# The first 16 tiles of the conditioning product: the conditions stationary in four column groups, the weights moving

## The chip, the cores and the metric

The kernel runs on one core of a Trainium2 chip. The metric is the device time of one execution in microseconds (us), the median of three runs. The core's engines are TensorE (PE; PEld is its weight load), VectorE (DVE), ScalarE (ACT), GpSimd (POOL) and SyncE (SP), which here issues most of the loads from HBM.

## What is computed

One inference step of a two-layer decoder trunk, for a prompt of 256 tokens and 8 samples of one token each (264 columns in all). Cut to the part in question:

```python
for l in range(DEPTH):                                   # DEPTH = 2
    mod = jax.nn.silu(c) @ W['w_mod'][l] + W['b_mod'][l] # c: (1 or 8, 1024), w_mod[l]: (1024, 6144)
    sh1, sc1, g1, sh2, sc2, g2 = split(mod, 6)
    h = rmsnorm(x, W['mix_pre_g'][l]) * (1 + sc1) + sh1
    z, xbc, dt_raw, u, v, ga, gb = split_cols(h @ W['w_in'][l], IN_SIZES)
    ...                                                  # SSD branch, gated MLP branch, merge
    x = x + g1 * rmsnorm(merged @ W['w_o'][l], W['mix_post_g'][l])
    h = rmsnorm(x, W['ffn_pre_g'][l]) * (1 + sc2) + sh2
    ...                                                  # dense (l = 0) or top-2-of-8 channel mixer (l = 1)
```

Everything is float32. The first 16 tiles of 128 columns of `w_mod[0]` give `sh1` and `sc1` of layer 0, and without them the first `h` can't be formed.

## The kernel before, in words

Activations lie with the features on the 128 partitions (8 tiles of 128 features, 264 columns). The large products split every weight chunk of 1024 by 256 into a high part (ScalarE, `split_hi`) and a low part (VectorE, `split_lo`), and TensorE multiplies the parts with those of the activations in `pe_phase` (lines 367, 368, 374). Each engine has its own program; semaphores tie them together, and each engine works through its program in the order in which it is written. There is no planner: the order is written out by hand.

The front of the kernel is what stands before the first of these products.

- SyncE loads the 9 conditions into `ctok`, then 8 pieces of `w_mod[0]`, each 1024 rows by 256 columns (1 MB, runs of 1 KB), into buffers that are free at that time (`START`: `zs`, `ub`, `vb`, `sga`, `sgb`, `hf` and two of the `raw` ring). After them on the same queue come the first two chunks of `w_in`; the third waits until VectorE has made the low part of chunk 0.
- ScalarE's queue loads x as rows of tokens; GpSimd's queue loads the parameter rows, the convolution state and small tables.
- TensorE turns the conditions (line 733), and ScalarE copies them to `cT` (line 1227). Then comes a loop over the 8 pieces. For each piece, `unit` (line 771) computes two tiles: for each of 8 row blocks the 128 by 128 block of `w_mod` is stationary and the ten condition columns, repeated up to 12 times, move. Between the pieces stand the transposes of x, of the parameters and of the states (`turn`, lines 748 to 760) and, after the seventh piece, the sum of squares for the first norm (`norm(1)`, line 716). All of that is one sequence on TensorE.
- VectorE copies each turned tile from PSUM (line 1577). When x is complete, ScalarE squares it; after the sum comes the root (ScalarE, line 1211), the reciprocal (VectorE, line 1515) and the scaling of x (line 1581).
- VectorE then takes the 16 tiles' sums from PSUM (`take`, line 1588), adds the bias and folds the norm's gain into the scale (`finish`, lines 1595 and 1598), and forms `h` (`modulated`, lines 1533 to 1538). ScalarE and VectorE split `h` (lines 1219 and 1520), and the first product starts.

The other 80 tiles of `w_mod` are computed by the same `unit` later, between the large products (`fill`), and are not touched by the diff.

Of the kernel before, what the change touches and what calls it, by code (L numbers as in the profile page):

```python
# [7 lines left out]
ALU = mybir.AluOpType  # L8
ACT = mybir.ActivationFunctionType
AX = mybir.AxisListType  # L10

P = 128
MT = 2
CW = MT * P
# [21 lines left out]
def hybrid_ssd_chunkmlp_moe_step(nc, A, O):  # L36
# [14 lines left out]
    KT = D // P  # L51
# [14 lines left out]
    NC = B + 2  # L66
# [13 lines left out]
    N0, Q0 = {}, {}  # L80
# [9 lines left out]
    for l in range(L):  # L90
        for name in ("xbc", "dt", "v", "u", "z", "ga", "gb"):
            k = IN_CHUNKS.get(name, 1)
# [28 lines left out]
    with ctx:  # L121
        def sb(name, shape, dt=F32, where=ctx):
# [6 lines left out]
        hf = sb("hf", [P, KT, T])  # L129
        rs = sb("rs", [P, 2, T])  # L130
        ident = sb("ident", [P, P])
# [6 lines left out]
        mod = sb("mod", [P, L, 6 * KT, NC])  # L138
# [14 lines left out]
        zs = sb("zs", [P, KT, T], F32, mixer)  # L153
        ub = sb("ub", [P, KT, T], F32, mixer)
        vb = sb("vb", [P, KT, T], F32, mixer)
        sga = sb("sga", [P, KT, T], F32, mixer)
        sgb = sb("sgb", [P, KT, T], F32, mixer)
# [8 lines left out]
        hT = sb("hT", [P, D], F32, mixer)  # L166
# [60 lines left out]
        raw45 = sb("raw45", [P, 2, KT * T])  # L227
# [4 lines left out]
        raw6 = raw + [b[:, 0:KT * CW].rearrange("p (k c) -> p k c", k=KT)  # L232
                      for b in (hf[:, :, :].rearrange("p k t -> p (k t)"), raw45[:, 0], raw45[:, 1])]

        ctok = xdt
        sq1 = xraw[:, 0:KT * T].rearrange("p (k t) -> p k t", k=KT)
        ptok = mix[:, :, :].rearrange("p h q -> p (h q)")
        stok = xc
# [10 lines left out]
        acc = ctx.enter_context(nc.psum_tensor("acc", [P, 4, 512], F32))  # L249
        ms = ctx.enter_context(nc.psum_tensor("ms", [P, 4, 512], F32))  # L250
# [3 lines left out]
        sem = {s: ctx.enter_context(nc.semaphore(s)) for s in SEMAPHORES}  # L254
# [6 lines left out]
        def row(name, l, k=None):  # L261
            r0, rows = ROWS[name]
            return PT[:, l, r0:r0 + rows] if k is None else PT[:, l, r0 + k:r0 + k + 1]

        def bc(ap, axis, shape):
            return ap.unsqueeze(axis).to_broadcast(shape)
# [182 lines left out]
        XT = 2 * NQ + 1  # L449
# [3 lines left out]

        GROUPS = [(0, r) for r in (0, 1, 2, 4, 3, 5)] + [(1, r) for r in (0, 1, 2, 4, 3, 5)]
        FIRST = 2 * KT
        FILL = ({"gb": 1, "vs": 1, "w_turned": 3, "diag": 1, "taken": 1, "mix0": 1, "y_taken": 1, "mix1": 1, "gate": 2,
# [20 lines left out]
        LANDED = [16 * (CLASS[:u + 1].count(CLASS[u]) + (1 if CLASS[u] < 4 else 0)) for u in range(NU)]  # L479
        f_in = [sem[f"f_in{j}"] for j in range(5)]  # L480

        START = [b[:, :, 0:CW] for b in (zs, ub, vb, sga, sgb, hf)] + raw6[4:6]
        START_IN = [sem[f"raw_full{s}"] for s in range(2, R6)] + f_in[0:4]


# [9 lines left out]
                          "norm3": q["gu"] + 1, "end": q["gu"] + EQ, "norm4": q["gu"] + EQ,  # L495
                          **{f"g{i}": q["gu"] + 2 * i + 1 for i in range(FP)}})
        assert Q0["xbc", 1] == Q0["gu", 0] + EQ
        RIDERS = {Q0["xbc", 0]: list(range(FIRST))}
        at = FIRST
        for l in range(L):  # L500
            for name, units in FILL[l].items():
# [23 lines left out]
        def _(sp):  # L525
# [1 line left out]
            sp.dma_start(ctok[0:1, :], A["c_prompt"]).then_inc(sem["c_in"], 16)  # L527
            sp.dma_start(ctok[1:1 + B, :], A["c_sample"]).then_inc(sem["c_in"], 16)
            wm = [A["w_mod"][l].rearrange("(k p) m -> p k m", p=P) for l in range(L)]
            for c in range(FIRST // MT):  # L530
                sp.dma_start(START[c], wm[0][:, :, CW * c:CW * (c + 1)]).then_inc(START_IN[c], 16)
            fed = 0

            def feed(to):
# [177 lines left out]
        def _(pe):  # L712
# [6 lines left out]
            def norm(v):  # L719
                for c in range(2):  # L720
                    if v == 1:
                        pe.wait_ge(sem["sq_ready"], squares(v) + c + 1)
                        ins = sum_tiles(sq1, ms[:, 3, 0:T], HT * c, HT * (c + 1))
                    else:
                        pe.wait_ge(sem["sq_folded"], folds(v) + c + 1)
                        ins = sum_tiles(hf, ms[:, 0, 0:T], HT * c, HT * c + HT // 2, last=HT + HT // 2)
                ins.then_inc(sem["ssq_ready"], 1)
# [8 lines left out]
            def turn(p):  # L736

                what, c, h = TURNS[p]
                bank = turn_bank(p)
                if p >= 2:  # L740
                    pe.wait_ge(sem["aux_copied"], p - 1)
                if what == "params":
                    pe.wait_ge(sem["params_in"], 16 * L * len(ROWS))
                    for l in range(L):
                        for r in range(RT):
                            rows = min(P, NROW - r * P)
                            c0 = (l * RT + r) * P
                            ins = pe.transpose(bank[:, l * NROW + r * P:l * NROW + r * P + rows],
                                               ptok[0:rows, c0:c0 + P], ident[0:rows, 0:rows])
                elif what == "state":  # L750
                    pe.wait_ge(sem["states_in"], 16 * L)
                    for k in range(CT):
                        ins = pe.transpose(bank[:, k * SR:(k + 1) * SR], stok[0:SR, c * CD + k * P:c * CD + (k + 1) * P],
                                           ident[0:SR, 0:SR])
                else:
                    pe.wait_ge(sem["x_in"], 16 * (NQ + 1))
                    rows = Q if c < NQ else B
                    for k in range(4 if c < NQ else KT):
                        f0 = c * D + (4 * h + k) * P
                        ins = pe.transpose(bank[:, k * rows:(k + 1) * rows], xtok[0:rows, f0:f0 + P],  # L760
                                           ident[0:rows, 0:rows])
                ins.then_inc(sem["aux_turned"], 1)

            def unit(v, q, weights):


                at = RIDERS[q].index(v)
                times = min(12, (512 - 272) // NC - at)
                out = mod_sums(q, at, times).rearrange("p (r c) -> p r c", c=NC)
                for k in range(KT):  # L770
                    ins = pe.matmul(out, weights(k), bc(cT[:, k, :], 1, [P, times, NC]), start=k == 0, stop=k == KT - 1)  # L771
                ins.then_inc(sem["f_used"], 1)
# [14 lines left out]
                filled += FILL[l][place]  # L787

            pe.wait_ge(sem["c_ready"], 1)
            for c in range(FIRST // MT):  # L790
                pe.wait_ge(START_IN[c], 16)
                for j in range(MT):
                    unit(MT * c + j, Q0["xbc", 0], lambda k: START[c][:, k, j * P:(j + 1) * P])
                if c <= XT:
                    turn(c)
                if c == XT + 1:
                    norm(1)
            for p in range(XT + 1, len(TURNS)):
                turn(p)

# [399 lines left out]
        def _(act):  # L1200
# [7 lines left out]
            def norm_rs(v):  # L1208

                act.wait_ge(sem["ssq_ready"], v)  # L1210
                act.activation(rs[:, 0, :], ms[:, 3 if v == 1 else 0, 0:T], ACT.Sqrt, bias=eps[:, 0:1],
                               scale=1.0 / D).then_inc(sem["root_ready"], 1)
# [8 lines left out]
            for c in range(NQ):  # L1221
# [2 lines left out]
            act.wait_ge(sem["c_in"], 32)  # L1224
            act.activation(ctok[0:NC, :], ctok[0:NC, :], ACT.Silu).then_inc(sem["c_silu"], 1)
            act.wait_ge(sem["c_turned"], 1)
            act.activation(cT[:, :, :], ms[:, 0, 0:KT * NC].rearrange("p (k c) -> p k c", k=KT), ACT.Copy) \
                .then_inc(sem["c_ready"], 1)
            act.wait_ge(sem["aux_copied"], XT)
            norm_sq(1, x)  # L1230
            norm_rs(1)
            for l in range(L):
                if l == 0:
                    split_hi(act, N0["xbc", 0], 0)
# [252 lines left out]
        def _(dve):  # L1487
# [4 lines left out]
            def then(ins):  # L1492

                nonlocal steps
                steps += 1
                ins.then_inc(sem["dve_chain"], 1)
                dve.wait_ge(sem["dve_chain"], steps)
# [60 lines left out]
                        .then_inc(sem["x_ready"], 1)  # L1558

            dve.memset(ctok[0:NC, :], 0.0).then_inc(sem["ctok_zero"], 1)  # L1560
            dve.memset(eps[:, :], EPS)
            then(dve.memset(ones[:, :], 1.0))

# [20 lines left out]
            def take(q, done):  # L1584

                dve.wait_ge(sem["f_used"], done)
                for to, sums in riders(q):
                    then(dve.tensor_copy(to, sums))

            def finish(*groups):  # L1590

                for g in groups:
                    l, r = GROUPS[g]
                    to = mod[:, l, r * KT:(r + 1) * KT, :]
                    then(dve.tensor_tensor(to, to, bc(row("b_mod", l)[:, r * KT:(r + 1) * KT], 2, [P, KT, NC]), ALU.add))
                    weight = row(("mix_pre_g", "mix_post_g", "ffn_pre_g", "ffn_post_g")[(0, 0, 1, 2, 2, 3)[r]], l)
                    if r % 3 == 1:
                        then(dve.scalar_tensor_tensor(out=to, in0=to, scalar=1.0, in1=bc(weight, 2, [P, KT, NC]),
                                                      op0=ALU.add, op1=ALU.mult))
                    if r % 3 == 2:  # L1600
                        then(dve.tensor_tensor(to, to, bc(weight, 2, [P, KT, NC]), ALU.mult))

            for l in range(L):
                take(Q0["xbc", l], (FIRST, FIRST + 48)[l])
                finish(6 * l, 6 * l + 1)
                modulated(l, 0, 4 * l + 1, 2 * l + 1)
                lo_of_x(5 * l + 1, hf)
                if l == 0:
# [484 lines left out]
```

## Time and the profile before

| | |
|---|---|
| median of 3 runs | 1934.86 us (1934.45 to 1938.47) |
| the profiled execution's own time | 1932.93 us |
| its span in the trace | 1931.2 us |
| mean granted TensorE clock | 0.971 of full |
| TensorE busy | 1831.0 us, 95% of the span |
| VectorE busy | 1346.2 us, 70% |
| ScalarE busy | 1004.9 us, 52% |
| moved by the DMA engines | 465.29 MB |

The span is the stretch from the first to the last recorded event; the execution's own time is a little longer. Times in the trace count from the span's start. A matmul's record covers its whole passage through the array, so records overlap, and the rate is read from the starts. An f32 matmul leaves two records; one on split operands leaves one.

### The profile page before, as it was taken

How to read it: one execution, taken by the hardware profiler on the slowest of the kernel's cores; microseconds unless marked ns; L12 is line 12 of the kernel's file. 1: busy time of each engine (PE TensorE's matmuls, PEld its weight loads, DVE VectorE, ACT ScalarE, POOL GpSimd, SP SyncE). 2: the span in 40 equal slices, each digit the busy share in tenths (PEclk: the TensorE clock that was granted, in tenths of full speed). 3: DMA queues.
4: the chain of work that ended last, by engine and by line, in shares of the span. 5: the costliest groups of instructions: out<-in, count | busy, mean ns of one | idle time of the engine just before them, and what ended most of it. 6: DMA issues, size and time to landing. Idle time of an engine off the chain costs nothing.

```text
span 1931.2 us, 34497 instructions
## 1 busy us (share of the span) xinstructions
PE 1831.0 (95%) x13768; PEld 1744.3 (90%) x13768; DVE 1346.2 (70%) x1654; ACT 1004.9 (52%) x983; POOL 63.7 (3%) x95
## 2 busy tenths in 40 slices
PE   8899989979999999999996899999999999999995
PEld 7899888979999999989895899989898989899994
DVE  1577857553444646775737798978887888888885
ACT  1455633333333345653332677767675767666772
POOL 4000200000000000020000000000000000000000
PEclk9999999999999999999997899999999999999997
DMA  8464854666665656683550999989998999999990
GB/s 256 132 209 151 262 156 141 186 184 196 189 195 171 180 154 209 192 275 113 153 164 19 349 356 339 361 279 355 336 357 301 313 342 348 349 308 358 340 338 23
DMA packets 421110, 465.29 MB, mean 241 GB/s; under 512 B 11043, under 2 KB 393203, under 8 KB 420978
## 3 DMA queue, kind: packets, MB, share of 16 engines
q1 hardware_dynamic: 413970, 441.65, 71.2%
q0 software_dynamic: 6720, 20.86, 3.5%
q8 instruction: 91, 1.49, 0.3%
q10 hardware_dynamic: 304, 1.08, 0.2%
q14 instruction: 25, 0.20, 0.0%
HBM read 452.84 MB, written 10.92 MB: 240 GB/s over the span
## 4 chain that ended last, share of the span: by engine, by line
PE 83%; DVE 9%; ACT 3%; DMA 2%; issue 2%; POOL 0%; SPq 0%; DVEq 0%; ACTq 0%; POOLq 0%
PE acc L367 9%; PE acc L368 9%; PE acc L374 9%; PE acc L1125 9%; PE acc L1129 9%; PE acc L1126 9%; PE acc L771 6%; PE acc L1158 4%; PE acc L1164 4%; PE acc L1159 4%; PE ms L716 1%; PE ms L1083 1%; ACT whi L307 1%; DVE wlo L312 1%; PE ms L1107 1%
## 5 line engine op out<-in xcount | busy, mean ns | idle before, releaser
L332 DVE TENSOR_TENSOR wlo<-raw,whi 128x2048 fp32r<-128x2048 f32 x220 | 503.8, 2292 | 90.8 <-ACT whi L327 90.0
L327 ACT ACTIVATE whi<-raw 128x2048 fp32r<-128x2048 f32 x220 | 420.7, 1913 | 79.2 <-PE acc L1164 73.8
L367 PE MATMUL acc<-xhi,whi 128*128 128x264 f32 x1584 | 406.4, 293 | 10.0 <-DVE xlo L1520 8.0
L312 DVE TENSOR_TENSOR wlo<-raw,whi 128x2048 fp32r<-128x2048 f32 x112 | 256.7, 2292 | 210.1 <-ACT whi L307 209.5
L368 PE MATMUL acc<-xlo,whi 128*128 128x264 f32 x1584 | 400.0, 289 | 0.0
L1125 PE MATMUL acc<-whi,hghi 128*128 128x256 f32 x1408 | 351.7, 288 | 3.5 <-issue 1.9
L1126 PE MATMUL acc<-whi,hglo 128*128 128x256 f32 x1408 | 345.2, 282 | 3.5 <-issue 3.5
L367 PEld LDWEIGHTS acc<-xhi,whi 128*128 128x128 f32 x1584 | 305.5, 193 | 17.2 <-issue 14.1
L368 PEld LDWEIGHTS acc<-xlo,whi 128*128 128x128 f32 x1584 | 306.1, 193 | 0.1
L1126 PEld LDWEIGHTS acc<-whi,hglo 128*128 128x128 f32 x1408 | 267.1, 190 | 4.1 <-issue 3.9
L1125 PEld LDWEIGHTS acc<-whi,hghi 128*128 128x128 f32 x1408 | 266.2, 189 | 4.8 <-issue 4.6
L307 ACT ACTIVATE whi<-raw 128x2048 fp32r<-128x2048 f32 x112 | 214.7, 1917 | 81.3 <-PE acc L374 66.5
L374 PE MATMUL acc<-xhi,wlo 128*128 128x264 f32 x1584 | 207.7, 284 | 0.0
L374 PEld LDWEIGHTS acc<-xhi,wlo 128*128 128x128 f32 x1584 | 198.5, 188 | 0.0
L1129 PE MATMUL acc<-wlo,hghi 128*128 128x256 f32 x1408 | 197.5, 282 | 0.0
L1129 PEld LDWEIGHTS acc<-wlo,hghi 128*128 128x128 f32 x1408 | 180.8, 189 | 0.0
L1158 PE MATMUL acc<-whi,gthi 128*128 128x512 f32 x352 | 139.9, 397 | 0.0
L1159 PE MATMUL acc<-whi,gtlo 128*128 128x512 f32 x352 | 139.1, 395 | 0.0
L332 DVE TENSOR_TENSOR wlo<-hf,whi 128x2048 fp32r<-128x2048 f32 x44 | 100.9, 2293 | 29.0 <-ACT whi L327 29.0
L327 ACT ACTIVATE whi<-hf 128x2048 fp32r<-128x2048 f32 x44 | 84.3, 1916 | 30.5 <-PE acc L1164 16.1
L771 PEld LDWEIGHTS acc<-cT,xraw 128*128 128x128 f32 x736 | 88.1, 197 | 9.5 <-DMA xraw<-in_w_mod_dram 6.6
L1164 PE MATMUL acc<-wlo,gthi 128*128 128x512 f32 x352 | 96.4, 395 | 0.0
(362 smaller groups left out, 2125.2 us busy)
## 6 DMA issues: line engine op xcount, KB each, us to landing
raw<-in_exp_wd_dram SPq DMA_DIRECT2D x76, 1024.0 KB, 5.6
raw<-in_exp_wg_dram SPq DMA_DIRECT2D x72, 1024.0 KB, 6.8
raw<-in_exp_wu_dram SPq DMA_DIRECT2D x72, 1024.0 KB, 7.3
raw<-in_w_in_dram SPq DMA_DIRECT2D x52, 1024.0 KB, 5.3
xraw<-in_w_mod_dram SPq DMA_DIRECT2D x46, 512.0 KB, 5.1
late<-in_w_mod_dram SPq DMA_DIRECT2D x34, 512.0 KB, 6.8
hf<-in_exp_wu_dram SPq DMA_DIRECT2D x16, 1024.0 KB, 7.0
hf<-in_exp_wg_dram SPq DMA_DIRECT2D x16, 1024.0 KB, 6.8
```

The source lines that it names most:

```text
L307: act.activation(whi[slot], raw[slot], ACT.Copy).then_inc(sem["hi_ready"], 1)
L312: dve.tensor_tensor(wlo[slot], raw[slot], whi[slot].bitcast(F32), ALU.subtract) \
L327: act.activation(whi[j % R3], raw6[slot], ACT.Copy).then_inc(sem["hi_ready"], 1)
L332: dve.tensor_tensor(wlo[j % R3], raw6[slot], whi[j % R3].bitcast(F32), ALU.subtract) \
L367: pe.matmul(out, a, hi(k), start=first and k == 0, stop=False)
L368: pe.matmul(out, a, lo(k), start=False, stop=False)
L374: ins = pe.matmul(out, b, hi(k), start=False, stop=last and k == nk - 1)
L1125: pe.matmul(out, hghi[:, k, half, :], whi[s][:, k, :], start=k == 0, stop=False)
L1126: pe.matmul(out, hglo[:, k, half, :], whi[s][:, k, :], start=False, stop=False)
L1129: ins = pe.matmul(out, hghi[:, k, half, :], wlo[s][:, k, :], start=False, stop=k == KT - 1)
L1158: pe.matmul(out, hi, wh[:, cols], start=d == 0 and k == 0, stop=False)
L1159: pe.matmul(out, lo, wh[:, cols], start=False, stop=False)
```

## The change

For the first 16 tiles the operands change places. The conditions, padded with zeros from 10 to 32 columns, are copied to `cwide` and become the stationary side. The weights move, 512 columns at a time. A piece is now one block of 128 rows by all 2048 columns (1 MB, runs of 8 KB), and its four matmuls write to the four groups of 32 partitions of one PSUM bank, each group 512 columns of the result. The eight pieces accumulate there, so a sum is complete only after the eighth. ScalarE copies the bank to `first`, TensorE turns it with four transposes into a second bank, and VectorE adds the bias for all 16 tiles in one operation (`finish_first`). The order of pieces, turns and the norm's sum on TensorE stays.

```diff
+        first = hT[:, 0:512]
+        cwide = hT[:, 512:768].rearrange("p (k c) -> p k c", k=KT)
...
-        START = [b[:, :, 0:CW] for b in (zs, ub, vb, sga, sgb, hf)] + raw6[4:6]
+        START = [b[:, :, :].rearrange("p k t -> p (k t)")[:, 0:FIRST * P] for b in (zs, ub, vb, sga, sgb, hf)] \
+            + [raw45[:, s, 0:FIRST * P] for s in range(2)]
...
-        RIDERS = {Q0["xbc", 0]: list(range(FIRST))}
+        RIDERS = {}
...
-            for c in range(FIRST // MT):
-                sp.dma_start(START[c], wm[0][:, :, CW * c:CW * (c + 1)]).then_inc(START_IN[c], 16)
+            for k in range(KT):
+                sp.dma_start(START[k], A["w_mod"][0, k * P:(k + 1) * P, 0:FIRST * P]).then_inc(START_IN[k], 16)
...
             pe.wait_ge(sem["c_ready"], 1)
-            for c in range(FIRST // MT):
-                pe.wait_ge(START_IN[c], 16)
-                for j in range(MT):
-                    unit(MT * c + j, Q0["xbc", 0], lambda k: START[c][:, k, j * P:(j + 1) * P])
-                if c <= XT:
-                    turn(c)
-                if c == XT + 1:
+            pe.wait_ge(sem["ctok_zero"], 2)
+            for k in range(KT):
+                pe.wait_ge(START_IN[k], 16)
+                for j in range(4):
+                    ins = pe.matmul(acc[32 * j:32 * (j + 1), 0, :], cwide[:, k, :], START[k][:, 512 * j:512 * (j + 1)],
+                                    start=k == 0, stop=k == KT - 1)
+                if k <= XT:
+                    turn(k)
+                if k == XT + 1:
                     norm(1)
+            ins.then_inc(sem["f_used"], FIRST // 2)
+            pe.wait_ge(sem["c_ready"], 2)
+            for i in range(4):
+                ins = pe.transpose(acc[:, 1, i * P:(i + 1) * P], first[:, i * P:(i + 1) * P], ident[:, :])
+            ins.then_inc(sem["f_used"], FIRST // 2)
             for p in range(XT + 1, len(TURNS)):
                 turn(p)
...
             act.wait_ge(sem["c_turned"], 1)
+            act.activation(cwide[:, :, 0:NC], ms[:, 0, 0:KT * NC].rearrange("p (k c) -> p k c", k=KT), ACT.Copy)
             act.activation(cT[:, :, :], ms[:, 0, 0:KT * NC].rearrange("p (k c) -> p k c", k=KT), ACT.Copy) \
                 .then_inc(sem["c_ready"], 1)
             act.wait_ge(sem["aux_copied"], XT)
             norm_sq(1, x)
             norm_rs(1)
+            act.wait_ge(sem["f_used"], FIRST // 2)
+            act.activation(first, acc[:, 0, :], ACT.Copy).then_inc(sem["c_ready"], 1)
...
             dve.memset(ctok[0:NC, :], 0.0).then_inc(sem["ctok_zero"], 1)
+            dve.memset(cwide[:, :, NC:32], 0.0).then_inc(sem["ctok_zero"], 1)
...
+            def finish_first():
+
+                dve.wait_ge(sem["f_used"], FIRST)
+                to = mod[:, 0, 0:FIRST, :].rearrange("p (j i) c -> p j i c", i=4)
+                bias = row("b_mod", 0)[:, 0:FIRST].rearrange("p (j i) -> p j i", i=4)
+                sums = acc[:, 1, :].rearrange("p (i j c) -> p j i c", i=4, c=32)[:, :, :, 0:NC]
+                then(dve.tensor_tensor(to, sums, bc(bias, 3, [P, 4, 4, NC]), ALU.add))
+                scale = mod[:, 0, KT:2 * KT, :]
+                then(dve.scalar_tensor_tensor(out=scale, in0=scale, scalar=1.0, in1=bc(row("mix_pre_g", 0), 2, [P, KT, NC]),
+                                              op0=ALU.add, op1=ALU.mult))
+
             for l in range(L):
-                take(Q0["xbc", l], (FIRST, FIRST + 48)[l])
-                finish(6 * l, 6 * l + 1)
+                if l == 0:
+                    finish_first()
+                else:
+                    take(Q0["xbc", l], FIRST + 48)
+                    finish(6 * l, 6 * l + 1)
```

## Rows read from the trace of the kernel before

**Rows 1.** The chain of waits, 0 to 70 us: start, us, what.

```profile
2.77 6.85 DMA zs<-in_w_mod_dram
...
9.75 5.81 PE acc L771 x32
...
36.65 3.75 PE acc L771 x32
40.40 3.59 PE ms L716 x16
...
48.76 0.25 DVE mod L1588
...
50.13 0.19 DVE hf L1533
...
54.53 0.56 PE acc L367
```

**Rows 2.** Stretches: length, busy time of each engine, granted clock, DMA share, GB/s.

```profile
15.30:40.20 24.90, 24.90 (x223) 24.40 (x222) 3.49 (x6) 3.34 (x3) 6.71 (x13) 1.00 1.04 315
54.50:58.20 3.70, 3.67 (x17) 3.70 (x18) 3.70 (x4) 1.64 (x1) 0.00 (x0) 0.50 0.02 4
...
1126.00:1130.00 4.00, 4.00 (x37) 4.00 (x36) 3.33 (x4) 3.35 (x3) 0.00 (x0) 1.00 1.03 395
...
1296.00:1330.00 34.00, 34.00 (x288) 34.00 (x288) 30.18 (x23) 24.80 (x24) 0.00 (x0) 1.00 1.06 343
9.60:34.50 24.90, 24.75 (x205) 24.65 (x206) 2.99 (x5) 2.05 (x2) 12.41 (x24) 1.00 1.10 330
```

**Rows 3.** Transfers issued from 0 to 60 us; last the median from issue to landing.

```profile
raw<-in_w_mod_dram SPq DMA_DIRECT2D x2, 1024.0 KB, 14.9
...
mix<-in_cmlp_ln_b_dram POOLq DMA_DIRECT2D x2, 4.0 KB, 5.1
```

**Rows 4.** Waits of SyncE's queue, 0 to 60 us: total, times, longest.

```profile
SPq L283 <- DVE wlo L312: 26.1, 1, 26.1
```

**Rows 5.** Timeline of TensorE in the scan of layer 0: start, us, what.

```profile
278.19 3.83 PE L933 MATMUL ms<-dth,ident 16*128 16x128 f32 x32
...
289.78 1.97 PE L945 MATMUL ms<-mix,xdt 128*64 128x128 f32 x32
291.68 1.98 PE L952 MATMUL ms<-xw,bt 128*128 128x512 f32 x4
...
317.15 0.44 PE L945 MATMUL ms<-mix,xdt 128*64 128x128 f32 x4
317.37 0.44 PE L947 MATMUL ms<-ce,hT 128*64 128x128 f32 x4
317.59 0.44 PE L945 MATMUL ms<-mix,xdt 128*64 128x128 f32 x4
```

**Rows 6.** Groups by shape on TensorE: busy us, mean ns of one, idle before.

```profile
L952 PE MATMUL ms<-xw,bt 128*128 128x512 f32 x16 | 7.9, 618 | 0.0
```

**Rows 7.** Timeline of the front and the first chunk, all engines.

```profile
8.98 0.24 ACT L1227 ACTIVATE cT<-ms 128x80 f32<-128x80 f32 x1 [1.17 <-PE ms L733]
...
15.36 0.51 POOL L654 DMA_DIRECT2D mix<-in_cmlp_ln_b_dram  x1
15.39 0.60 PE L760 MATMUL ms<-ident,xraw 128*128 128x128 f32 x4
...
16.11 0.69 DVE L1577 COPY x<-ms 128x512 f32<-128x512 f32 x1 [13.96 <-PE ms L760]
16.21 8.32 SPq L531 DMA_DIRECT2D raw<-in_w_mod_dram  x2
...
44.39 1.90 ACT L307 ACTIVATE whi<-raw 128x2048 fp32r<-128x2048 f32 x1
...
62.33 0.37 ACT L404 ACTIVATE mod<-acc 128x80 f32<-128x80 f32 x2 [6.20 <-PE acc L374]
62.59 0.62 ACT L1240 ACTIVATE xraw<-acc 128x528 f32<-128x528 f32 x1
```

## The prediction, made before the changed kernel was run

> **What bounds the kernel now.** I read the chain of waits over the first 70 us first, because the diff touches only what stands before the first product of the input projection. [rows 1] is that chain. The reader should see that from 9.75 us on it is TensorE in nearly every row: a piece of w_mod (32 records, 3.75 us), a turned tile of x or the parameters, the next piece, and last the sum of squares, 40.40 + 3.59 = 43.99 us. From there it goes to the root on ScalarE, over VectorE (reciprocal, scaling, modulation), and back to TensorE at 54.53 us, 10.54 us after the norm's sum ended.
>
> The stretches confirm it [rows 2]: between 15.30 and 40.20 us TensorE is busy for 24.90 of 24.90 us. The transfers are not what it waits for. The chain has piece 1 landing at 2.77 + 6.85 = 9.62 us. Pieces 7 and 8 are issued from 16.21 us on and take a median of 14.9 us to land [rows 3, 7]: piece 7 at about 31.1 us, while TensorE takes it up at 36.65 us. So TensorE is about 5.5 us behind the data by then; the arithmetic of the front bounds it, the transfers stand close behind.
>
> What is won in the front is not given back: SyncE's next load of w_in waits 26.1 us for VectorE's low half of chunk 0 [rows 4], so the stream behind is released by the first product and moves with it.
>
> **The matmuls.** Removed are 8 pieces of 32 records, 120 columns or fewer moving over 128 stationary ones. Added per piece are 4 matmuls of 512 moving columns over 32 stationary ones; an f32 matmul leaves two records in this trace (16 for the 8 matmuls of the norm), so 8 records. Their cost one by one: four f32 records of 512 columns take 1.98 us and one lasts 0.618, so they start (1.98 - 0.618) / 3 = 0.454 us apart [rows 5, 6]. Serially a piece is 8 x 0.454 = 3.63 us, no better than the 3.75 it replaces. Everything hangs on whether the four column groups work at once.
>
> No row shows groups of 32. The nearest are the state products, 64 stationary columns that go to partitions 0 and 64 in turn: 32 records of 128 columns take 1.97 us, 0.062 us each, where 32 records of 128 columns through the whole width take 3.83 us, 0.120 us each [rows 5]. That is 1.94 times the rate: two groups overlap wholly. In the second chunk each group gets four records in a row before the other group's turn, and 8 records still take 0.44 us, 0.055 each [rows 5], so the overlap doesn't depend on a strict change of group. I therefore take four at once: 3.63 / 4 = 0.91 us a piece. The bounds are this and 3.63 (no overlap); two at a time would be 1.82.
>
> The Trainium skill (TensorE: Matmul & The Clock Gate, Measured speedup vs the span model) gives 2.38 times for three column groups at 512 columns. By that efficiency of 0.79 I estimate 1.15 us a piece in place of 0.91, and the sum would be 0.24 us later. The rows for two groups show no such loss.
>
> **The clock.** TensorE granted half the clock, the 1.2 GHz level, from 54.50 to 58.20 us after it had stood idle, and the full 2.4 GHz in the busy stretch [rows 2]. Piece 1 shows the same: 5.81 us against 3.75 [rows 1]. A front that waits for data in each piece may stay at the lower level: 1.82 us a piece, still less than a piece's transfer. I take the lower level up to piece 7 (the front begins in it and is then busy for less than now), and let it end as it does at 58.20: 3.7 us after work without gaps begins. Piece 7 takes 1.82 of those, 1.88 us of the norm run at half speed (0.94 us of its work) and 3.59 - 0.94 = 2.65 at full: 4.5 us. The bounds of the norm are 3.59 and 7.18.
>
> The Trainium skill (the same page, Loop structure matters more than you think) warns of just this loop: bursts of matmuls with a wait for a transfer between them run cold. By that rule a piece is 1.82 us and not 0.91; had I gone by the busy stretch alone, the sum would end 1.8 us earlier, the full-clock rival below.
>
> **The transfers.** Eight of 1 MB remain, with rows of 8 KB in place of 1 KB. Over 9.60 to 34.50 us the queues moved 330 GB/s. Experts' down weights, 4 KB rows, move at 395 in a dense stretch; gate and up weights, 1 KB rows, at 343 [rows 2]. I take the ratio 1.15 for 8 KB too: piece 7 lands at 9.62 + (31.1 - 9.62) / 1.15 = 28.3 us. Bounds: 31.1 (no gain) and 9.62 + 21.5 x 330 / 395 = 27.6. Piece 1 I leave at 9.62, since x's 1 MB is in flight with it.
>
> **The smaller parts.** The extra copy of the conditions on ScalarE, like the present 0.24 us one [rows 7], delays TensorE from 9.22 to 9.46 us, which the landing at 9.62 hides; uncovered it is 0.24. The extra memset delays only two memsets of constants on VectorE, which has no work in the front until 16.11 us [rows 7]. After piece 8 come a copy of 512 columns on ScalarE (0.62 for 528), four transposes (0.60, both [rows 7]) and three handovers, about 0.1 each by the gaps of the chain: 0.91 + 0.62 + 0.60 + 0.3 = 2.4 us after the norm's sum. VectorE is busy on the norm's branch until 48.76 - 43.99 = 4.77 us after it, so all of this hides, with 2.4 us to spare; if piece 8 took 3.63 it would end at 5.15 and 0.4 would show. Behind the copy on ScalarE waits the first high half (1.9 us, done now by 46.3 us [rows 7]): it would end 0.91 + 0.1 + 0.62 + 1.9 = 3.5 us after the sum, before the modulated x needs ScalarE. VectorE's five small operations from 48.76 to 50.13 (1.37 us) become two: one of 160 columns from PSUM, between 0.25 (a row of the chain with 80) and 0.69 (512 [rows 7]), by the slope 0.33 + 0.03, and one of 0.27: 0.63. That saves 0.74. ScalarE's two copies of sums at 62.33 us vanish; they stood behind 6.20 us of idle time [rows 7], so that is worth nothing.
>
> **The sum.** Piece 7 lands at 28.3, + 1.82 + 4.5 = 34.6 us for the norm's sum, + 10.54 - 0.74 = 44.4 us for the first product, 10.1 us before 54.53. The profiled execution would go from 1932.93 to 1922.8 us. It lies 1.93 us under the median of the runs, 1934.86, so I forecast 1924.8 us for the median.
>
> **Rivals.**
> *Full clock.* If bursts of 0.91 us and a transpose per 2.7 us of transfer keep the clock, the sum is 28.3 + 0.91 + 3.59 = 32.8, first product at 42.6, 11.9 us won: 1923.0. For it: the array streams four groups at once. Against: the rows after idle time.
> *Transfers no faster.* The end of the load at 395 GB/s belongs to 4 KB rows in another phase; here parameters travel in small rows beside it. Piece 7 at 31.1: 37.4, 47.2, 7.3 us won: 1927.5. The same result follows if the parameters, issued until 15.36 us and landing 5.1 us later [rows 3, 7], wait so long behind 8 KB rows that their turn holds piece 7 up; that begins when they take over 12 us.
> *No overlap.* With four groups one after another a piece and its transpose cost 3.63 + 0.44, what they cost now (4.0). TensorE stays the bound: + 0.6 us over seven pieces, + 0.4 for the late sums, - 0.74: 1935.1, no change. The two-group rows speak against it.
> *Slower: records that drain.* If each record of a column group had to finish before the next could start, it would cost its full 0.618 us [rows 6], not 0.454: 4.94 + 0.44 a piece, 1.3 us more than now, in place at every piece of the front. Seven pieces make + 9, the late sums + 1.7, less 0.74: 1944.8. It decides from a piece of about 4 us up. Against it: the state products start every 0.06 us, which leaves no room for a record to finish first.
>
> **How the numbers follow.** Forecast 0.42, full clock 0.25, transfers no faster 0.20, no overlap 0.08, draining 0.05. A change of 0.2%, 3.9 us, is about what a measurement of this kernel can tell from none. The first three give faster, 0.87; no overlap is same, 0.08; draining is slower, 0.05. The range leaves the last two out: down to 1920.5 (full clock with the transfers' upper bound, 12.6 us, and the run-to-run spread), up to 1930 (slow transfers and a norm wholly at the lower clock, 7.3 - 2.7 = 4.6 us won).
>
> **What the profile after would show.** Piece 7 landing near 28 us and no longer waited for by 5 us of queued work; TensorE idle between pieces with a transfer as releaser; eight 512-column records per piece starting well under 0.45 us apart; the clock at 0.5 in those stretches or not; the norm's sum ending near 34.6 and the first product at 44.4; the sums' transposes done before VectorE asks. Records 0.45 apart, or a wait at the parameters' turn, would make the prediction wrong.

## The result and the profile after

Four runs of the changed kernel have a median of 1919.68 us (1918.42 to 1921.63); four runs of the kernel before on the same chip have one of 1936.66. The ratio is 0.9911, with a 95% interval from 0.989 to 0.9932: 17 us faster, and at least 13. That is more than the forecast of 1924.8 and just beyond its range. The profiled execution took 1918.42 us, its span is 1916.6 (1931.2 before), its mean granted clock 0.967.

The chain of waits of the changed kernel over its first 60 us answers to [rows 1]. Columns: start, us, what.

```profile
6.07 22.14 DMA raw<-in_w_mod_dram
28.25 1.93 PE acc L799 x8
30.18 4.79 PE ms L721 x16
35.00 0.49 ACT rs L1223
...
39.74 0.34 DVE mod L1625
...
40.38 0.19 DVE hf L1548
...
44.78 0.56 PE acc L369
```

The row of pieces on TensorE is gone. One transfer, that of piece 7, now carries the chain up to 28.25 us, and TensorE, VectorE and the first product follow it. The first product starts 54.53 - 44.78 = 9.75 us earlier.

Stretches of the same kernel, beside [rows 2] (length; busy time of PE, PEld, DVE, ACT and POOL, each with its number of records; granted clock; DMA share; GB/s):

```profile
15.00:20.00 5.00, 3.52 (x26) 1.16 (x24) 2.08 (x3) 0.00 (x0) 5.00 (x11) 1.00 1.03 397
20.00:25.00 5.00, 3.09 (x24) 0.92 (x24) 0.23 (x1) 2.78 (x3) 1.94 (x3) 0.70 1.04 323
25.00:30.00 5.00, 3.56 (x16) 0.92 (x12) 0.50 (x1) 0.56 (x1) 0.00 (x0) 0.50 1.02 340
9.60:28.20 18.60, 13.81 (x76) 4.44 (x68) 3.49 (x6) 3.34 (x3) 12.34 (x24) 0.83 1.03 368
```

TensorE is no longer full in the front, the DMA engines are, and the granted clock falls from full to half between 20 and 25 us. Over the front the queues move 368 GB/s, where they moved 330.

Transfers issued in the first 60 us, against [rows 3], and the wait of SyncE's queue against [rows 4]:

```profile
raw<-in_w_mod_dram SPq DMA_DIRECT2D x2, 1024.0 KB, 23.3
mix<-in_cmlp_ln_b_dram POOLq DMA_DIRECT2D x2, 4.0 KB, 7.4
```

```profile
SPq L285 <- DVE wlo L314: 29.5, 3, 21.4
```

The last two pieces are both issued early now and take 23.3 us from issue to landing; the parameters' rows take 7.4 us in place of 5.1, which holds nothing up. SyncE's longest wait is still one for the low half of a chunk, 21.4 us.

The timeline of TensorE and of the late sums in the same front, against [rows 5, 7]:

```profile
9.38 1.94 PE L799 MATMUL acc<-zs,hT 128*32 128x512 f32 x8 [0.46 <-ACT cT L1240]
...
17.43 1.07 PE L799 MATMUL acc<-sga,hT 128*32 128x512 f32 x8 [0.57 <-DMA sga<-in_w_mod_dram]
18.43 0.66 PE L765 MATMUL ms<-ident,xraw 128*128 128x128 f32 x4
...
28.25 1.93 PE L799 MATMUL acc<-raw,hT 128*32 128x512 f32 x8 [1.44 <-DMA raw<-in_w_mod_dram]
...
34.89 1.06 PE L799 MATMUL acc<-raw,hT 128*32 128x512 f32 x8
36.03 0.60 ACT L1246 ACTIVATE hT<-acc 128x512 f32<-128x512 f32 x1 [0.55 <-PE acc L799]
36.68 0.66 PE L808 MATMUL acc<-ident,hT 128*128 128x128 f32 x4 [0.72 <-ACT hT L1246]
```

Eight records of 512 columns take 1.00 us at the full clock (17.43 to the transposes at 18.43) and 1.93 at the lower one. The late sums are turned at 36.68 + 0.66 = 37.34 us; VectorE asks for them at 39.74.

So the front is nearly as forecast, and 4.9 us of the 14.6 by which the span is shorter come from elsewhere. The stretches of both kernels cut at the same events show where. They are cut at the first product, at the first matmul that gathers the tokens of an expert, and at the last that scatters results back. The middle and the experts, first in the kernel before:

```profile
54.50:1067.30 1012.80, 955.73 (x7541) 924.09 (x7541) 612.27 (x1096) 417.12 (x498) 41.02 (x47) 0.96 0.58 175
1067.30:1904.10 836.80, 827.27 (x5864) 775.51 (x5864) 705.74 (x509) 573.42 (x471) 0.00 (x0) 0.99 0.98 328
```

And the changed kernel:

```profile
44.80:1058.90 1014.10, 957.88 (x7540) 926.70 (x7541) 613.09 (x1096) 416.74 (x497) 40.92 (x47) 0.96 0.58 175
1058.90:1888.50 829.60, 824.10 (x5863) 772.75 (x5864) 704.87 (x509) 573.23 (x471) 0.00 (x0) 1.00 0.99 331
```

By stage: the front -9.75, the middle (all between the first product and the experts) +1.3, the experts -7.2, and the tail, from there to the ends of the spans at 1931.2 and 1916.6, 28.1 for 27.1: +1.0. The sum is -14.6. No line of the experts' loop is in the diff, and its number of TensorE's records is the same but for one. Yet it is 7.2 us shorter, and its clock 1.00 in place of 0.99.

The waits of TensorE say where. The loop over the experts runs three times over two experts each and so jumps back twice. The waits around the first jump, in the kernel before (us in total, times, longest):

```profile
PE acc L1126 <- issue: 1.6, 1, 1.6
PE acc L1125 <- issue: 1.0, 1, 1.0
```

In the changed kernel, around the same jump (line 1137 is 1125 there):

```profile
PE acc L1137 <- issue: 0.9, 1, 0.9
```

"issue" means that nothing in the trace was waited for. The timeline of the kernel before at its second jump shows that the second wait falls in the middle of a row of matmuls that have all they need, behind the first five matmuls after the jump, and that the clock is low after it:

```profile
1490.30 0.38 PE L1125 MATMUL acc<-whi,hghi 128*128 128x256 f32 x1 [0.91 <-issue]
...
1490.88 0.28 PE L1125 MATMUL acc<-whi,hghi 128*128 128x256 f32 x1
1493.02 0.58 PE L1126 MATMUL acc<-whi,hglo 128*128 128x256 f32 x1 [1.87 <-issue]
1493.40 0.42 PE L1125 MATMUL acc<-whi,hghi 128*128 128x256 f32 x1
...
1498.74 0.30 PE L1126 MATMUL acc<-whi,hglo 128*128 128x256 f32 x1
```

From 1493.40 to 1498.74 us the matmuls start 0.21 us apart and not 0.12, the lower level of the clock. The sum for the loop: waits of 1.0 + 1.6 + 0.9 + 1.9 = 5.4 us against 1.4 in the changed kernel, 4.0 us, and 5.3 us of work at 0.21 for 0.12, about 2.3 us more. That is 6.3 of the 7.2.

### The profile page after: what moved, and what is told of

It is laid out like the page before. It is cut to its first block, busy times and chain, and to the rows that moved or that the text cites. A ratio compares the mean times of both kernels' runs of the same rounds, so it can differ in the third digit from the quotient of the medians.

```text
span 1916.6 us, 34119 instructions
## 1 busy us (share of the span) xinstructions
PE 1815.9 (95%) x13580; PEld 1717.4 (90%) x13580; DVE 1345.9 (70%) x1652; ACT 1005.1 (52%) x983; POOL 63.6 (3%) x95
## 4 chain that ended last, share of the span: by engine, by line
PE 81%; DVE 10%; DMA 4%; ACT 3%; issue 2%; SPq 0%; POOL 0%; ACTq 0%; DVEq 0%; POOLq 0%
PE acc L369 9%; PE acc L370 9%; PE acc L1137 9%; PE acc L1141 9%; PE acc L1138 9%; PE acc L376 9%; PE acc L1170 4%; PE acc L1176 4%; PE acc L1171 4%; PE acc L776 4%; PE ms L721 1%; ACT whi L309 1%; DVE wlo L314 1%; PE ms L1095 1%; DMA raw<-in_w_mod_dram 1%
## 5 line engine op out<-in xcount | busy, mean ns | idle before, releaser
L329 ACT ACTIVATE whi<-raw 128x2048 fp32r<-128x2048 f32 x220 | 420.7, 1913 | 78.8 <-PE acc L1176 73.8
```

The lines of the kernel that those rows point to most:

```text
L329: act.activation(whi[j % R3], raw6[slot], ACT.Copy).then_inc(sem["hi_ready"], 1)
```

## The experiments

The theory: the removed matmuls make TensorE's program 376 instructions shorter ahead of the experts' loop, so the loop's head lies at another place in the blocks in which instructions are loaded, and the waits behind the jump hang on that place. The page of the profile has the queue that loads instructions; packets, MB, share of 16 engines' span; first before:

```profile
q8 instruction: 91, 1.49, 0.3%
```

And after:

```profile
q8 instruction: 86, 1.41, 0.3%
```

Both give 16.4 KB for a packet. The Trainium skill (Runtime: NRT & Kernel Launch, Instruction fetch mechanics) says that instructions come in blocks of 256, loaded in sequence, and that a taken branch to a block that isn't held makes the engine wait for a load; packets and waits here agree with that. Counted in the program with blocks of 256, the loop's head stands 14 TensorE instructions ahead of a block's end before the change and 134 after it. (376 is 256 + 120.) Those 14 are the five matmuls between the two waits of the kernel before, two instructions each, and four waits on semaphores. The count is mine; where the waits of the next kernels fall tests it.

The rival: the loop gains because everything in front of it ends earlier, or stands differently in time, by the change itself. The ratios of the first two kernels below, of the one column group and of the 1 KB rows stand against 22 runs of the kernel before with a median of 1937.14 us, those of the other four against 7 with 1935.82.

**The changed kernel with the loop put back in its place.** Sixty transposes, of two instructions each, stand in a branch that is never taken, ahead of the loop. What is executed is the changed kernel.

```diff
                 with pe.If(crowded(pe)):
+                    for k in range(60):
+                        pe.transpose(ms[:, 0, 0:P], x[:, 0, 0:P], ident[:, :])
                     all_tokens(pe, expert)
```

> The changed kernel with 60 transposes added in the branch of the mixer that this data never takes (120 TensorE instructions, never executed). The change made TensorE's program 376 instructions shorter ahead of the expert loop; 376 is 256 + 120, so the padding puts the loop's head back where it stood before the change, counted in the 16 KB blocks (256 instructions) in which the trace shows instructions being fetched. Theory of the place: the expert loop loses again what it gained behind the front, two waits for issue at each jump back instead of one, so about 1925 us, 4 to 6 us over the changed kernel, with the first product still at 44.8 us. Rival (chance, or the start 10 us earlier, made the expert loop faster): as the changed kernel, 1919.7 us within 2 us, with one wait per jump back.

Measured: 1928.52 us (1924.48 to 1933.99), ratio 0.9956 (0.9941 to 0.9971). Against the 0.9911 of the changed kernel that loses 0.45%, some 8.7 us, more than the theory had expected. The waits of its first jump and its stretches (middle, experts):

```profile
PE acc L1140 <- issue: 2.1, 1, 2.1
PE acc L1139 <- issue: 0.8, 1, 0.8
```

```profile
44.50:1061.90 1017.40, 961.13 (x7540) 929.33 (x7541) 612.27 (x1096) 417.14 (x497) 41.02 (x47) 0.96 0.58 174
1061.90:1898.00 836.10, 826.24 (x5863) 774.51 (x5864) 704.94 (x508) 573.31 (x471) 0.00 (x0) 0.99 0.98 329
```

Both waits are back, and the experts take 836.1 us, 6.5 more than in the changed kernel; the first product stays at 44.5. In its profile the middle is 3.3 us longer too, of which more below.

**The kernel before with the loop moved to its new place**, by 68 such transposes, and nothing else.

```diff
                 with pe.If(crowded(pe)):
+                    for k in range(68):
+                        pe.transpose(ms[:, 0, 0:P], x[:, 0, 0:P], ident[:, :])
                     all_tokens(pe, expert)
```

> The kernel before with 68 transposes added in the branch never taken (136 instructions), which moves the expert loop to the place that it has in the changed kernel and changes nothing that is executed. Theory of the place: 4 to 6 us faster than before, about 1931 us, first product unchanged at 54.5 us, one wait for issue per jump back. Rival: as before, 1936 us within the spread of its runs, two waits per jump back.

Measured: 1928.63 us (1927.04 to 1933.88), ratio 0.9962 (0.9946 to 0.9978): 7.4 us won without a change to anything that is executed. The wait of its first jump and the stretches (middle, experts):

```profile
PE acc L1127 <- issue: 0.6, 1, 0.6
```

```profile
55.10:1068.30 1013.20, 955.65 (x7541) 924.53 (x7541) 612.51 (x1096) 416.82 (x498) 40.94 (x47) 0.96 0.58 175
1068.30:1898.20 829.90, 824.28 (x5864) 772.89 (x5864) 705.53 (x509) 573.33 (x471) 0.00 (x0) 1.00 0.99 331
```

The experts take 829.9 us, as in the changed kernel, with the front of the kernel before. With that the rival is out: the loop's gain doesn't come from the front.

**Another place.** If the second wait is tied to the end of a block, a head some 40 instructions ahead of one must have it behind about the 18th matmul (16 with the high half of the weights, two with the low one). With 47 transposes, 94 instructions, the head has 134 - 94 = 40 left; the expectation says 41.

```diff
                 with pe.If(crowded(pe)):
+                    for k in range(47):
+                        pe.transpose(ms[:, 0, 0:P], x[:, 0, 0:P], ident[:, :])
                     all_tokens(pe, expert)
```

> The changed kernel with 47 transposes in the branch never taken. In the kernel before, the second wait at a jump back comes after 5 matmuls, 14 instructions behind the loop's head; the changed kernel has 134 instructions there up to the end of the fetched block. This kernel has 41. Theory of the place: the second wait comes behind the 18th or 19th matmul of the loop, and is shorter, 0.2 to 1.2 us, since TensorE runs some 1.6 us longer while the next block is on its way; 1 to 4 us over the changed kernel if the clock holds, 6 to 8 if the wait takes the clock down. Rival (any shift of the code costs): two waits as long as in the kernel before, at the same matmul.

The timeline of its first jump:

```profile
1279.80 0.38 PE L1139 MATMUL acc<-whi,hghi 128*128 128x256 f32 x1 [0.73 <-issue]
...
1281.82 0.40 PE L1143 MATMUL acc<-wlo,hghi 128*128 128x256 f32 x2
1283.00 0.98 PE L1143 MATMUL acc<-wlo,hghi 128*128 128x256 f32 x6 [0.78 <-issue]
```

The wait stands behind the 18th matmul, the second of the eight with `wlo`, and is shorter, 0.78 us for 1.6 to 2.6, with more work standing between the jump and the block's end. At the second jump of this kernel no wait of its own is left; there the eight matmuls with `wlo` take 1.32 us (1488.68 to 1490.00), where the changed kernel needs 0.96 for them. So the place of the second wait is shown to follow the block.

The trace also has every load on the instruction queue, with its start and length. In the kernel before one starts at the second jump between 1490.5 and 1490.6 us (packets, MB, time as a share of 16 engines over that 0.1 us, which makes 1.10 us):

```profile
q8 instruction: 1, 0.02, 68.8%
```

It runs from 1490.57 to 1491.67 us, and the matmuls go on at 1493.02. The same holds for all five second waits of the kernels so far: a load of 16 KB starts 0.2 to 1.0 us after the first matmul behind the jump, and the matmuls go on 1.26 to 1.50 us after its end (here 1280.42 to 1281.50, then 1283.00). The changed kernel makes that load too, from 1480.18 to 1481.22 us at its second jump, but its matmuls run on through it. So the second wait goes with the load of the next block, and it is covered where enough instructions of the first block are left. What TensorE does in the 1.3 to 1.5 us between the load's end and the next matmul, no row names.

The experts take 829.9 us here too (stretches of the middle and the experts):

```profile
44.00:1065.10 1021.10, 961.17 (x7541) 929.45 (x7541) 613.20 (x1096) 417.86 (x497) 40.94 (x47) 0.95 0.57 174
1065.10:1895.00 829.90, 823.11 (x5864) 771.29 (x5864) 704.17 (x507) 571.93 (x471) 0.00 (x0) 1.00 0.99 331
```

The time, 1925.56 us (1921.64 to 1927.59), ratio 0.9944 (0.9928 to 0.9961), is nevertheless 6 us longer than the changed kernel's, where 1 to 4 were expected. In its profile that isn't the loop: the middle took 1021.1 us, 7 more.

**One column group for all four matmuls**, in four banks, so that they can't work at once; the copy of the bank becomes four copies.

```diff
-                    ins = pe.matmul(acc[32 * j:32 * (j + 1), 0, :], cwide[:, k, :], START[k][:, 512 * j:512 * (j + 1)],
+                    ins = pe.matmul(acc[0:32, j, :], cwide[:, k, :], START[k][:, 512 * j:512 * (j + 1)],
...
-            act.activation(first, acc[:, 0, :], ACT.Copy).then_inc(sem["c_ready"], 1)
+            for j in range(4):
+                ins = act.activation(first[32 * j:32 * (j + 1), :], acc[0:32, j, :], ACT.Copy)
+            ins.then_inc(sem["c_ready"], 1)
```

> The changed kernel, but all four matmuls of a piece use the first column group and go to four banks, and the copy to SBUF is four copies of 32 partitions. If the groups overlap and this is what makes the pieces cheap, a piece now costs 8 x 0.454 = 3.6 us at the full clock, TensorE is the bound of the front again, the norm's sum ends at about 44 us and the first product comes at about 54 to 55 us: the front's 9.8 us are lost and the time is about 1929 to 1930 us. Rival, that fewer instructions or the swap of operands alone makes it cheap: a piece stays near 1 to 2 us and the first product near 45 us.

Measured: 1930.27 us (1926.97 to 1934.36), ratio 0.9968 (0.9956 to 0.998). Its timeline:

```profile
15.18 3.62 PE L799 MATMUL acc<-ub,hT 128*32 128x512 f32 x8
...
55.46 0.56 PE L369 MATMUL acc<-xhi,whi 128*128 128x264 f32 x1 [2.48 <-DVE xlo L1537]
```

A piece takes 3.62 us for 1.07, TensorE bounds the front again, and the first product stands at 55.46, 0.9 us behind the kernel before. The whole front is lost; part of that are the four copies, which take 2.4 us in place of 0.6 and lie on the chain here. The 6 us by which the kernel still lies below the kernel before are the place of the loop, which it shares with the changed kernel: its experts take 830.0 us.

**The pieces in rows of 1 KB**, into the same buffers.

```diff
-        START = [b[:, :, :].rearrange("p k t -> p (k t)")[:, 0:FIRST * P] for b in (zs, ub, vb, sga, sgb, hf)] \
-            + [raw45[:, s, 0:FIRST * P] for s in range(2)]
+        START = [b[:, :, 0:CW] for b in (zs, ub, vb, sga, sgb, hf)] \
+            + [raw45[:, s].rearrange("p (k t) -> p k t", k=KT)[:, :, 0:CW] for s in range(2)]
...
-                sp.dma_start(START[k], A["w_mod"][0, k * P:(k + 1) * P, 0:FIRST * P]).then_inc(START_IN[k], 16)
+                sp.dma_start(START[k], A["w_mod"][0, k * P:(k + 1) * P, 0:FIRST * P].rearrange("p (a c) -> p a c", c=CW)).then_inc(START_IN[k], 16)
...
-                    ins = pe.matmul(acc[32 * j:32 * (j + 1), 0, :], cwide[:, k, :], START[k][:, 512 * j:512 * (j + 1)],
+                    ins = pe.matmul(acc[32 * j:32 * (j + 1), 0, :], cwide[:, k, :], START[k][:, 2 * j:2 * (j + 1), :],
                                     start=k == 0, stop=k == KT - 1)
```

> The changed kernel, but each piece lands in rows of 1 KB (256 columns, then a gap of 8 in the buffer) instead of 8 KB; the matmuls are the same. If long rows made the transfers faster, as the prediction took with a ratio of 1.15, piece 7 is taken up at about 31 us instead of 28.25, the first product comes at 47 to 48 us instead of 44.8, and the time is about 2.8 us over the changed kernel, 1922.5 us. If the transfers are limited by something else, everything stays within 1 us of the changed kernel.

Measured: 1923.22 us (1922.28 to 1928.07), ratio 0.9936 (0.9915 to 0.9957); first product at 47.98, 3.2 us later. Stretches of this kernel and of the changed one over the same time, and this kernel's piece 7:

```profile
9.60:20.00 10.40, 8.09 (x44) 2.40 (x44) 2.08 (x3) 0.00 (x0) 10.40 (x21) 1.00 1.11 344
```

```profile
9.60:20.00 10.40, 8.91 (x48) 2.79 (x40) 2.77 (x4) 0.00 (x0) 10.40 (x22) 1.00 1.03 399
```

```profile
31.43 1.93 PE L799 MATMUL acc<-raw,hT 128*32 128x512 f32 x8
```

The 8 KB rows move 399 / 344 = 1.16 times as fast, and piece 7 comes at 28.25 in place of 31.43 us. In the whole time the intervals don't separate the two kernels; the gain is read from the front of the traces.

**The norm's sum ahead of piece 7**, since it needs only x and TensorE stands idle there.

```diff
-                if k == XT + 1:
+                if k == XT:
                     norm(1)
```

> The changed kernel with the norm's sum of squares moved ahead of piece 7: it follows the parameters' turn, where its squares have been ready since 24.3 us, instead of waiting behind a piece that lands at 28.2. If the chain reads rightly (the last wait is the landing of piece 7, then piece, norm, root), the norm's sum ends near 31.5 us instead of 35.0 and the first product comes at 41.3 to 42 us instead of 44.8, about 3 us won: 1916.5 us. Rival: pieces 7 and 8 and the turn of the sums, which now follow the norm, set the end in its place, and less than 1 us is won.

Measured: 1917.68 us (1916.47 to 1918.77), ratio 0.9909 (0.9892 to 0.9925). The first product starts at 40.32 us, 4.5 earlier and a microsecond before the time expected, and the time is 2 us shorter than the changed kernel's, which the intervals don't separate. Stretches of the middle and the experts:

```profile
40.30:1058.70 1018.40, 960.71 (x7541) 929.03 (x7541) 613.17 (x1096) 418.23 (x497) 41.02 (x47) 0.96 0.58 174
1058.70:1886.80 828.10, 823.39 (x5864) 772.03 (x5864) 704.90 (x508) 572.07 (x471) 0.00 (x0) 1.00 0.99 331
```

In this profile the middle is 4.3 us longer than in the changed kernel's, about as much as the front wins.

**Useless matmuls to hold the clock.** Five of 512 columns behind the turned states, ahead of the first product; their results are read by nobody, and a never-taken branch keeps the loop's place.

```diff
             for p in range(XT + 1, len(TURNS)):
                 turn(p)
+            for i in range(5):
+                pe.matmul(acc[:, 3, :], ident[:, :], START[0][:, 0:512], start=True, stop=True)
...
                 with pe.If(crowded(pe)):
+                    for k in range(118):
+                        pe.transpose(ms[:, 0, 0:P], x[:, 0, 0:P], ident[:, :])
                     all_tokens(pe, expert)
```

> The changed kernel with five matmuls of 512 columns without use, into a bank that nobody reads, on TensorE behind the states' turn (39 to 44 us), where it stood idle before the first product; 118 never-taken transposes keep the expert loop's place. If the idle time is what takes the clock to the lower level at the first products (0.22 us apart for 4.5 us instead of 0.12), they now run at 0.12 from the start or soon after, and the second chunk starts about 2 us earlier: 1917.5 us. Rival: the level stays low for the first products, nothing is won, 1919.7 us, or up to 0.5 us is lost where the extra matmuls end too late.

Measured: 1921.51 us (1919.22 to 1924.78), ratio 0.9932 (0.9916 to 0.9949). The first products do start 0.12 us apart from the first on, in place of 0.22 up to 49.3 us, but the middle takes 1017.1 us against 1014.1 in this profile, and in the time nothing is won.

**The best of both**: the norm early, one useless matmul behind each of pieces 3 to 6 and four behind the states.

```diff
+                if 2 <= k <= XT:
+                    pe.matmul(acc[:, 3, :], ident[:, :], START[k][:, 0:512], start=True, stop=True)
-                if k == XT + 1:
+                if k == XT:
                     norm(1)
...
             for p in range(XT + 1, len(TURNS)):
                 turn(p)
+            for i in range(4):
+                pe.matmul(acc[:, 3, :], ident[:, :], START[0][:, 0:512], start=True, stop=True)
...
                 with pe.If(crowded(pe)):
+                    for k in range(112):
+                        pe.transpose(ms[:, 0, 0:P], x[:, 0, 0:P], ident[:, :])
                     all_tokens(pe, expert)
```

> The changed kernel with the norm's sum ahead of piece 7, one matmul without use after the turns behind pieces 3 to 6, four behind the states' turn, and 112 never-taken transposes that keep the expert loop's place. If the front waits for the norm and the clock only, the norm runs at the full clock and ends at 29 to 30 us, the first product comes at 39 to 40 us and runs at the full clock: 4 to 5 us from the front, 2 from the first products, about 1913 us. Rival: the extra matmuls delay the turns or the pieces and take back what the clock gives: 1917 us or more.

Measured: 1916.76 us (1916.45 to 1919.66), ratio 0.9907 (0.9891 to 0.9924). Its timeline:

```profile
27.53 3.72 PE L721 MATMUL ms<-xraw,ones 128*128 128x264 f32 x16
...
41.06 0.36 PE L369 MATMUL acc<-xhi,whi 128*128 128x264 f32 x1 [1.36 <-DVE xlo L1541]
41.26 0.28 PE L370 MATMUL acc<-xlo,whi 128*128 128x264 f32 x1
```

The norm's sum is at the full clock (3.72 us against 4.79), the first product 3.7 us earlier than in the changed kernel and at the full clock; the time is the lowest of all, 3 us under the changed kernel's, from which the intervals don't separate it. The 1913 us that were expected were not reached.

**What stays open: the middle.** It took 1012.8 to 1013.2 us in the three kernels whose first product stands behind 54 us, and 1014.1 to 1021.1 in the others. The changed kernel and the two that only put a longer never-taken branch into it execute the same work there, and it took 1014.1, 1017.4 and 1021.1 us. TensorE's busy time for the same records is 957.9, 961.1 and 961.2 us, all of the first difference and half of the second; the granted clock is 0.96, 0.96 and 0.95. Each has one profile, and the 22 runs of the kernel before alone lie between 1932.05 and 1942.83 us, with mean granted clocks of 0.967 to 0.973. So it stays open how much belongs to the kernel and how much to the execution, and whether an earlier first product is the cause.

## Why the prediction was wrong in the size

The front came out by its own steps:

| step | forecast | measured |
|---|---|---|
| a piece at the full clock | 0.91 | 1.00 (17.43 to 18.43) |
| a piece at the lower clock | 1.82 | 1.93 (28.25 to 30.18) |
| piece 7 taken up | 28.3 | 28.25 |
| the norm's sum takes | 4.5 | 4.79 |
| the norm's sum ends | 34.6 | 34.97 |
| late sums ready after that | 2.4 | 2.37 (37.34) |
| VectorE's two operations | 0.63 | 0.64 (39.74 to 40.38) |
| norm's sum to first product | 9.80 | 9.81 |
| first product | 44.4 | 44.78 |
| all that follows | 0 | -4.9 |

**Overlap.** Four groups do work at once: 3.56 us a piece in one group (15.18 to the transposes at 18.74), 1.00 in four, both from start to next start. The Trainium skill's figure for three groups (TensorE: Matmul & The Clock Gate, Measured speedup vs the span model), from which the prediction had the estimate of 1.15, lies above the 1.00, the 0.91 from the rows below it. "Draining" fell too: even one group alone took 3.56 us a piece, near the sum by [rows 5, 6] (3.63), and not 4.94. "No overlap" fell, but what its kernel measured was 0.9968 and not the 1.0 of the rival, for the reason that follows.

**Transfers.** The ratio of 1.15 that was taken from other rows is 1.16 here; "transfers no faster" is what the 1 KB kernel does, and its first product at 47.98 is near the rival's 47.2.

**Clock.** Neither of the two pure cases: pieces 3 to 5 ran at the full clock, 1, 2, 6 and 7 at the lower one, and the norm's sum paid 4.79 us. The Trainium skill (TensorE: Matmul & The Clock Gate, Loop structure matters more than you think) has a loop with a long wait for a transfer ahead of each matmul run at the lower clock. With waits of 0.6 to 1.7 us ahead of pieces 4 to 7 the trace agrees for pieces 6 and 7, not for 4 and 5; in all, four of these seven pieces ran at the lower clock.

**Small things.** The first piece was released at 9.38 us by ScalarE's copy and not by its transfer, as the prediction had it; as piece 7's transfer sets the end, it cost nothing.

**The step that failed** is the last one of the sum: "The profiled execution would go from 1932.93 to 1922.8 us", with "What is won in the front is not given back ... the stream behind is released by the first product and moves with it". It prices the diff by what is executed and takes all else for unchanged. But 188 matmul records less, with a weight load each, are also 376 instructions less in TensorE's program, and a loop a thousand microseconds later lay better for it. The sum had put that at nothing; it is 7.2 us in the trace, and 7.4 us when the old kernel is given the place alone. With the place undone the change measured 0.9956, 8.5 us, where the forecast had 10.1: that kernel lies within the range. In the profile the middle and the tail, 1.3 and 1.0 us longer, hide part of the loop's gain; without them the forecast would have been off by more. No rival had this mechanism, though the waits for "issue" of 1.6 and 1.9 us in the middle of a row of matmuls stood in the trace of before; I had read the stages that the diff touches and no other.

## What to carry to other kernels

When a change alters the number of instructions ahead of a hardware loop, look in the trace for waits on "issue" just behind the loop's jumps: their place moves with the program, and here they, and the lower clock after one of them, were worth 7 of 17 us. Such a gain can be had alone, here by 136 instructions in a branch that is never taken, and a change should be compared with the loop held in one place, or it is credited with what isn't its own. For this product with few stationary columns, moving the large operand over four column groups made a piece cheaper than its transfer (1.0 to 1.9 us for 1 MB), and after that the transfers bounded the front: rows of 8 KB in place of 1 KB were worth 3 us of it.

## What the runs showed of the hardware

- A jump back came with a wait of 0.3 to 1.1 us at every place that was tried, and a second one where a block of instructions ends soon after: 1.6 to 2.6 us when that is 14 instructions on, 0.8 and less at some 40, none seen at 134.
- The first matmul behind a jump back started 1.7 to 2.1 us after the end of a 16 KB load on the instruction queue, at all 20 such jumps of the ten profiles; the matmul behind a second wait 1.3 to 1.5 us after the end of the next load, at all five.
- After second waits of 1.87, 2.09 and 2.56 us TensorE worked at its lower clock for some microseconds; after 0.78 it did not. In the kernel before the drop followed its second jump (1.87) and not its first (1.60).
- Four column groups of 32 work at once even though an f32 matmul leaves two records in a row in one group: 8 records of 512 columns in 1.00 us against 3.56 in one group.
- 8 KB rows against 1 KB rows on the same loads: 399 against 344 GB/s, from 9.6 to 20 us.
- The same executed instructions took between 1014 and 1021 us in the middle of the kernel in single profiles of three programs that differ only in a branch that is never taken.
